# Another order and other operations in the opening of a two-block transformer kernel

## The reference, cut to what matters

```python
def rmsnorm(x, g):                       # x * rsqrt(mean(x*x) + eps) * g
...
cos, sin = rope_tables(positions)        # angle = position * inv (8 frequencies)
cond = jax.nn.silu(c)                    # 1 x 1024
for l in range(DEPTH):
    mod = (cond @ ada_w[l] + ada_b[l])[:, None, :]        # 1 x 6144
    sh1, sc1, g1, sh2, sc2, g2 = jnp.split(mod, 6, axis=-1)
    h = rmsnorm(x, norm1_g[l]) * (1 + sc1) + sh1
    x = x + g1 * hybrid_mixer(h, cos, sin, w_in[l], b_in[l], rel_bias[l], ...)   # first: h @ w_in + b_in
    h = rmsnorm(x, norm2_g[l]) * (1 + sc2) + sh2
    x = x + g2 * swiglu(h, w_ffn_in[l], w_ffn_out[l])
```

## Time and profile before

| | us |
|---|---|
| median of 3 runs (lowest, highest) | 1459.61 (1456.82, 1460.19) |
| the profiled execution | 1456.65 |
| its span, first to last instruction | 1454.8 |
| PE busy | 1432.1 (98%) |
| POOL busy | 1210.1 (83%) |
| ACT busy | 755.6 (52%) |
| DVE busy | 723.9 (50%) |

### The profile page before, as it was taken

One profiled execution on the slowest core, in us unless ns is written; L12 is line 12 of the kernel. 1 busy time (PEld: TensorE's weight loads), 2 busy tenths in 40 slices (PEclk: granted clock), 3 DMA queues, 4 the chain that ended last, 5 costly groups with the idle time before them and its releaser, 6 DMA issues.

```text
span 1454.8 us, 21549 instructions
## 1 busy us (share of the span) xinstructions
PE 1432.1 (98%) x7600; PEld 1199.7 (82%) x7600; DVE 723.9 (50%) x1557; ACT 755.6 (52%) x1272; POOL 1210.1 (83%) x984
## 2 busy tenths in 40 slices
PE   7999999999999999999999999999999999999997
PEld 5898777799988987778888888778888888788886
DVE  7863654766643754745566304454650044655202
ACT  4435774644444445765544445674654346655431
POOL 3899989888878986559898997966999977789994
PEclk9999999999999999999999999999999999999999
DMA  9994547689875996337676565644566755456651
GB/s 362 402 354 159 199 168 225 230 292 327 313 265 168 401 319 200 117 99 232 219 242 201 187 204 169 191 142 145 189 195 197 222 162 181 131 164 198 199 197 52
DMA packets 149415, 313.35 MB, mean 215 GB/s; under 512 B 10918, under 2 KB 31802, under 8 KB 149307
## 3 DMA queue, kind: packets, MB, share of 16 engines
q1 hardware_dynamic: 147552, 310.62, 63.8%
q10 hardware_dynamic: 1756, 1.35, 0.3%
HBM read 310.87 MB, written 1.06 MB: 214 GB/s over the span
## 4 chain that ended last, share of the span: by engine, by line
PE 92%; DVE 4%; ACT 1%; POOL 1%; DMA 1%; issue 1%; SPq 0%; DVEq 0%; ACTq 0%
PE bank L789 58%; PE bank L834 12%; PE bank L835 8%; PE bank L832 5%; PE bank L997 1%; PE bank L981 1%; POOL lo_units L733 1%; PE bank L870 1%; PE bank L967 1%; DMA x_rows<-in_x 1%; PE bank L1078 1%; PE bank L1013 1%; PE bank L1049 1%; PE bank L1039 0%; PE bank L1092 0%
## 5 line engine op out<-in xcount | busy, mean ns | idle before, releaser
L733 POOL TENSOR_TENSOR lo_units<-raw_units,hi_units 128x512 fp32r<-128x512 f32 (+3 forms) x928 | 1151.4, 1276 | 221.7 <-ACT hi_units L1371 220.6
L1371 ACT ACTIVATE hi_units<-raw_units 128x1024 fp32r<-128x1024 f32 (+1 forms) x470 | 482.6, 1030 | 411.1 <-PE bank L789 251.9
L789 PE MATMUL bank<-hi_units,turned 128*128 128x512 f32 (+3 forms) x1600 | 441.2, 390 | 1.2 <-DVE turned L1897 0.7
L789 PEld LDWEIGHTS bank<-hi_units,turned 128*128 128x128 f32 x1600 | 291.7, 189 | 53.5 <-issue 3.3
L835 PE MATMUL bank<-turned,lo_units 128*128 128x256 f32 x1024 | 288.0, 281 | 0.0
L789 PE MATMUL bank<-hi_units,turned_wide 128*128 128x512 f32 x992 | 274.5, 391 | 0.0
L834 PE MATMUL bank<-turned,hi_units 128*128 128x512 f32 x736 | 259.2, 397 | 0.0
L789 PE MATMUL bank<-lo_units,turned 128*128 128x512 f32 (+3 forms) x800 | 252.8, 383 | 0.9 <-POOL lo_units L733 0.5
L789 PEld LDWEIGHTS bank<-hi_units,turned_wide 128*128 128x128 f32 x992 | 185.3, 188 | 38.4 <-issue 0.5
L835 PEld LDWEIGHTS bank<-turned,lo_units 128*128 128x128 f32 x1024 | 194.4, 190 | 0.2
L789 PEld LDWEIGHTS bank<-lo_units,turned 128*128 128x128 f32 x800 | 149.7, 188 | 30.6 <-POOL lo_units L733 3.7
(11 more groups left out here) (261 smaller groups left out, 1288.6 us busy)
## 6 DMA issues: line engine op xcount, KB each, us to landing
ada_units<-in_ada_w SPq DMA_DIRECT2D x88, 512.0 KB, 7.8
raw_units<-in_w_ffn_tiles SPq DMA_DIRECT2D x72, 512.0 KB, 5.2
raw_units<-in_mlp_w_out SPq DMA_DIRECT2D x64, 512.0 KB, 3.3
raw_units<-in_mlp_w_tiles SPq DMA_DIRECT2D x56, 512.0 KB, 3.2
raw_units<-in_w_in SPq DMA_DIRECT2D x56, 458.0 KB, 9.7
raw_units<-in_w_in SPq DMA_DIRECT2D x48, 512.0 KB, 6.9
raw_units<-in_w_ffn_out SPq DMA_DIRECT2D x44, 512.0 KB, 3.5
raw_units<-in_moba_w_qkv SPq DMA_DIRECT2D x24, 512.0 KB, 3.7
```

The source lines that it names most:

```text
L733: pool.tensor_tensor(LO[:, s, b, 0:w], RAW[:, u["slot"], b, 0:w], HI_[:, s, b, 0:w].bitcast(F32), ALU.subtract).then_inc(lo_ready.sem, lo_ ...
L789: ins = pe.matmul(BANK[2 * c["pair"] + t][:, 0:w], (A[a] if A is BT else A[:, a])[:, part, t * P:(t + 1) * P], W[:, s, b, 0:w], start=(i = ...
L1371: act.activation(HI_[:, s, 0:n, 0:w], RAW[:, u["slot"], 0:n, 0:w], ACT.Copy)\
```

## The change

- The gain row and the whole bias row are brought first on ACT's queue, and one function, `constant_columns`, turns both into 24 columns by 24 one-column matmuls at the very start of TensorE's list. ACT copies them to SBUF (L1692 in the new numbering), ahead of its table load and of the squares. No tile is cleared any more, and DVE's sums of three chunks start by a plain multiply.
- `angles()` moves to the front of DVE's list, ahead of the first sums, and both sines to the front of ACT's, ahead of that copy. `tables()` moves ahead of `first_columns(0)`, and the issue of `rel_scratch` behind `first_hi(0)`.
- Unit 1 of shift 0 (chunk 0) leaves DVE too. It and unit 1 of scale 1 (chunk 3) are multiplied with the column of `cond` as the stationary operand and 512 columns moving, which gives a row (`sum_row`); ACT copies the row (`keep_sum_row`), and `column_sums` adds it by 4 more one-column matmuls.
- DVE makes the gained scale in `scale_columns` ahead of the reciprocal, so that only one addition is left between the sums of the shift and their use.
- The k-tiles of the first products go through ACT and DVE singly, and TensorE starts on each of them alone (`first_unit`).
- One unit, c1's unit 1, moves ahead of the sums of shift 1, and two fillers follow those sums.

TensorE's list from its start: in the kernel before,

The core of the diff; the removed lines of these functions stand in the kernel before, above, and the functions that are new are whole but for `first_turn` (the eight transposes of a half in one go) and `keep_sum_row` (one copy of a row of 512 by ACT):

```diff
-PE_UNITS = {(0, 3, 1)}
+PE_UNITS = {(0, 0, 1), (0, 3, 1)}
...
+        def constant_columns():
+            pe.wait_ge(first_gain_in, 16)
+            pe.wait_ge(first_bias_in, 16)
+            for j in range(3 * KT):
+                row = BIAS_ROW[:, j * P:(j + 1) * P] if j < 2 * KT else GAIN_ROW[:, (j - 2 * KT) * P:(j - 2 * KT + 1) * P]
+                ins = pe.matmul(columns[:, j:j + 1], row, ONES[0:1, 0:1], start=j == 0, stop=j == 3 * KT - 1)
+            ins.then_inc(product.sem, product.mark("constant columns"))
+        def sum_row(c, i, bank):
             u = c["units"][i]
             pe.wait_ge(ada_in[u["home"]][u["slot"]], 16 * (u["turn"] + 1))
             for k in range(UNIT_K):
+                kt = i * UNIT_K + k
+                ins = pe.matmul(bank[0:1, :], COND[:, kt:kt + 1], ada_raw(u)[:, k, :], start=k == 0, stop=k == UNIT_K - 1)
             ins.then_inc(ada_multiplied.sem, ada_multiplied.mark(u["index"]))
         def column_sums(c):
             n, half = c["key"][2], c["key"][2] % 2
             at = (KT if n >= 2 else 0) + 4 * half
             pe.wait_ge(ada_used.sem, ada_used.at(c["units"][-1]["index"]))
+            if n in SUM_ROW:
+                pe.wait_ge(act_side.sem, act_side.at(("sum row", n)))
+            if n < 2:
+                pe.wait_ge(rows.sem, rows.at(("scales", half)))
             for j in range(4):
+                if n in SUM_ROW:
+                    pe.matmul(columns[:, at + j:at + j + 1], SUM_ROW[n][:, j * P:(j + 1) * P], ONES[0:1, 0:1], start=j == 0, stop=False)
                 ins = pe.matmul(columns[:, at + j:at + j + 1], MOD[:, n * CW + j * P:n * CW + (j + 1) * P], ONES[:, 0:1],
+                                start=n not in SUM_ROW and j == 0, stop=j == 3)
+            ins.then_inc(product.sem, product.mark(("columns", n)))
...
+        def first_unit(c, i):
+            for m in range(UNIT_K):
+                pe.wait_ge(turned_lo.sem, turned_lo.at((("n1", 0), i * UNIT_K + m)))
+                unit(c, i, HT, only=m)
...
+        constant_columns()
         pe.wait_ge(ada_in[scale0["units"][0]["home"]][scale0["units"][0]["slot"]], 16)
+        keep_running(2)
+        pe.wait_ge(act_side.sem, act_side.at("constant columns"))
+        column_sums(scale0)
         keep_running(1)
+        sum_row(shift0, 1, BANK[2])
         for l in range(DEPTH):
             if l == 0:
                 tag = ("n1", l)
                 c0, c1 = todo.pop(0), todo.pop(0)
+                first_turn(0)
                 keep_running(1)
                 column_sums(shift0)
                 keep_running(2)
+                first_unit(c0, 0)
+                first_unit(c0, 1)
+                sum_row(scale1, 1, BANK[3])
+                first_turn(1)
+                column_sums(scale1)
                 unit(c1, 0, HT)
+                unit(c1, 1, HT)
                 column_sums(shift1)
+                keep_running(2, BANK[SB_[0]])
+                first_unit(c0, 2)
+                first_unit(c0, 3)
+                unit(c1, 2, HT)
+                unit(c1, 3, HT)
...
+            whole(b)
+            hi(a, rows)
+            hi(b, act_side)
+            hi(c, rows)
+            act.wait_ge(turned_lo.sem, turned_lo.at((("n1", 0), b)))
+            whole(d)
+            hi(d, act_side)
...
+        act.dma_start(GAIN_ROW, dram["norm1_g"][0:1, :]).then_inc(first_gain_in, 16)
+        act.dma_start(BIAS_ROW, dram["ada_b"][0:1, 0:4 * CW]).then_inc(first_bias_in, 16)
         act.dma_start(POS[:, :], dram["positions"].rearrange("b (t p) -> (b p) t", p=P),
                       allow_slow_non_contiguous=True).then_inc(pos_in, 16)
         act.wait_ge(c_in, 16)
         act.activation(CT, COND, ACT.Tanh, scale=0.5).then_inc(act_side.sem, act_side.mark("cond"))
+        act.dma_start(RB[:, :], dram["rel_bias"].rearrange("l h r -> (l h) r")).then_inc(rel_in, 16)
+        for what, dst in (("sin", SIN), ("cos", COS)):
+            act.wait_ge(rows.sem, rows.at(what))
+            act.activation(dst, dst, ACT.Sin).then_inc(act_side.sem, act_side.mark(what))
+        act.wait_ge(product.sem, product.at("constant columns"))
+        act.activation(MX[:, 0:3 * KT], BANK[SB_[1]][:, 0:3 * KT], ACT.Copy).then_inc(act_side.sem, act_side.mark("constant columns"))
         act.wait_ge(const_in, 16)
         bring_root_table(("n1", 0))
...
         unit_rows(0)
+        keep_sum_row(0, 1, BANK[2])
         unit_rows(1)
         prep(2)
         for l in range(DEPTH):
             if l == 0:
                 first_hi(0)
+                act.wait_ge(rows.sem, rows.at("rel"))
+                act.dma_start(scratch[:, :], RE[:, :]).then_inc(scratch_in, 16)
+                prep(3)
+                keep_sum_row(3, 1, BANK[3])
                 prep(NH)
                 first_hi(1)
                 prep(NH + 3)
...
+        def scale_columns(half):
+            columns, cols = BANK[SB_[1]], slice(4 * half, 4 * half + 4)
+            at = slice(KT + 4 * half, KT + 4 * half + 4)
+            dve.wait_ge(act_side.sem, act_side.at("constant columns"))
+            dve.wait_ge(product.sem, product.at(("columns", 2 + half)))
+            link(v.scalar_tensor_tensor(GAINED[:, cols], columns[:, at], 1.0, BIAS[:, at], ALU.add, ALU.add))
+            say(v.tensor_tensor(GAINED[:, cols], GAINED[:, cols], GAIN[:, cols], ALU.mult), ("scales", half))
...
+            say(v.tensor_tensor(SHIFT[:, cols], columns[:, cols], BIAS[:, cols], ALU.add), ("columns", half))
+            dve.wait_ge(turned.sem, turned.at((("n1", 0), half)))
+            whole(a)
+            lo(a)
+            lo(b)
+            whole(c)
+            lo(c)
+            lo(d)
...
+        angles()
         sums_upto(5)
+        scale_columns(0)
         dve.wait_ge(act_side.sem, act_side.at(("root", ("n1", 0))))
         say(v.reciprocal(RR[:, 0:NT], RSTD), "inverse root")
-        sums_upto(8)
+        sums_upto(7)
+        tables()
         for l in range(DEPTH):
             if l == 0:
                 first_columns(0)
-                sums_upto(15)
+                sums_upto(13)
+                scale_columns(1)
+                sums_upto(14)
                 first_columns(1)
-                tables()
-                angles()
```

More of the change, by code:

```diff
@@ L1200, in column_sums, with first_turn @@
-            if n < 2:
-                ins.then_inc(product.sem, product.mark(("columns", half)))
-        def keep_running(n):
+                                start=n not in SUM_ROW and j == 0, stop=j == 3)
+            ins.then_inc(product.sem, product.mark(("columns", n)))
+        def first_turn(half):
+            pe.wait_ge(act_side.sem, act_side.at(("unit rows", half)))
+            if half:
+                for k in (2, 3):
+                    pe.wait_ge(turned_lo.sem, turned_lo.at((("n1", 0), k)))
+            for k in range(4 * half, 4 * half + 4):
+                for t in range(NT):
+                    at = k % 4 // 2 * S + t * P
+                    ins = pe.transpose(BANK[(TQ, TP)[k % 2]][:, at:at + P], O[:, t, k * P:(k + 1) * P], con("ident"))
+            ins.then_inc(turned.sem, turned.mark((("n1", 0), half)))
@@ L1221, in _ @@
                 c0, c1 = todo.pop(0), todo.pop(0)
-                ready = lambda g: (act_side, ("unit rows", g // 2))
-                turn(tag, O, range(4), 0, ready)
-                turn(tag, O, range(4), 1, ready)
+                first_turn(0)
                 keep_running(1)
@@ L1932, in first_columns @@
[L1932 to L1938 removed]
+            a, b, c, d = range(4 * half, 4 * half + 4)
+            raw = lambda k: BANK[(TQ, TP)[k % 2]][:, k % 4 // 2 * S:(k % 4 // 2 + 1) * S]
```

101 lines of the change are left out of this document (23 added, 78 removed).

## The result

The changed kernel takes 1463.34 us (median of 6 runs, 1462.60 to 1464.30); the kernel before took 1459.37 beside it (6 runs, 1456.82 to 1460.99). The medians are 4.0 us apart, a quotient of 1.0027; the ratio on record, which isn't the quotient of the medians, is 1.0033 with an interval of 1.0021 to 1.0044. Either way the changed kernel is slower, by 4 to 5 us. The forecast was 1463.5.

A forecast was written before the change was run, and what follows sets the result against it. TensorE, busy 98% of the span, was taken to bound the kernel behind 52.19 us, a chain of waits the opening; 3.4 + 0.85 - 0.3 = +3.95 us on the median 1459.61 gave 1463.5, range 1458.0 to 1468.5.

The forecast's parts named there:

- The constant columns: Start of TensorE's list: 48 slow passes, 10.5 us, hold up ACT; the reciprocal ends at 20.3, 4.6 us later.
- Rival C: Opening: the column passes turn fast under way, end near 10 us and cost no wait; -1.4 us, 1458.2; chance 0.10.
- Rival B: Opening: the clock rises later, so scale 0's sums, a filler and much of the row sum take double; +5.5 to +7; chance 0.22.
- Who comes last: Ahead of the sums of shift 0: TensorE comes last at 24.35, DVE's last sum ends at 23.45; 0.9 us apart.
- First product: End of the opening on TensorE: the first product comes at 28.0 us, 3.4 later than before.
- The sums of shift 0: TensorE ahead of the first product: 16 passes instead of half as many, 1.8 to 1.95 us, ending at 26.2.
- The hand-over: From the sums of shift 0 to the first product: 1.85 us with single k-tiles instead of 3.06, saving 1.2.
- From the first product to the third chunk: TensorE's stretch up to the third column chunk: 28.4 us against 27.55, 0.85 later; bounds -1.0 and +2.0.
- The wait at c0's unit 3: Ahead of the third chunk: TensorE waits for ACT's rounding of weights; 0.8 us together with POOL's subtraction.
- The term of -0.3: Behind 52.19 us: TensorE's wait of about 0.3 us for POOL's remainders goes.
- What costs nothing: DVE's opening: the twelve operations of the angles take 2.5 us, hidden under the constant columns and the fillers.
- Rival D: Opening: POOL's first subtractions come 5 us later, and a wait of 3.3 for weights reaches TensorE; +7.3, 1466.9; chance 0.10.

The follow-up runs named there:

- shift_unit_on_dve: The changed kernel with unit 1 of shift 0 summed by DVE again, without its row sum on TensorE; 1464.77 us, ratio 1.0039.
- copy_late: The changed kernel with ACT's copy of the columns behind the root, and DVE's reciprocal and sums ahead of its scale columns; 1465.59 us, ratio 1.0045.
- before_again: The kernel before, run again with no edit; 1459.77 us, ratio 1.0002.
- one_constant: The changed kernel with one matmul of 24 columns in place of the 24 one-column matmuls, leaving gain and bias out; 1461.03 us, ratio 1.0020.
- filler_first: The changed kernel with the first two fillers ahead of the constant columns; 1468.34 us, ratio 1.0060.
- rows_only: The kernel before with both units as row sums and the sums of scale 1 ahead of c1's unit 0; 1461.24 us, ratio 1.0007.
- more_fillers: The kernel before with one more filler behind the sums of scale 0 and one more ahead of those of shift 0; 1457.66 us, ratio 0.9994.
- split_constants: The changed kernel with twelve of the constant columns at the start and twelve behind the first four products; 1466.67 us, ratio 1.0048.

## Why the prediction was right, and which terms were off

The total (+3.95 forecast, +4.0 between medians) and the sign hold, and so does the mechanism up to the first product. The stretch behind it was mis-sized beyond its own bounds, and the total came out by luck. Taken step by step:

- **The constant columns.** Right within 0.2 us: 48 passes from 4.39 to 14.69 (4.2 to 14.7 forecast), squares at 16.41 (16.5), fillers to 18.26 (18.3), sums of scale 0 to 19.63 (19.6), reciprocal to 20.34 (20.3). Rival C is refuted: 10.3 us of passes without a pause stayed at 0.216 us each. This disagrees with the rule of the Trainium skill, "TensorE: Matmul & The Clock Gate", Part 1, that the warm-up is a budget of time and not a number of matmuls. The prediction took these times from the trace and not from that page. Rival B did not come in the changed kernel's two profiles; in `shift_unit_on_dve`, whose list is the same up to there, one execution shows part of it (the filler behind the sums takes 2.05 and the transposes 1.97, where the changed kernel has 1.10 and 1.09).
- **Who comes last.** "It is TensorE and no longer DVE that comes last, by 0.9": by 0.73 in the trace (DVE done at 23.49, TensorE there at 24.22), and shown by `copy_late`, where DVE's reciprocal comes 3.8 us earlier and TensorE gains nothing by it. `shift_unit_on_dve` shows how near DVE is: with two sums more it is the last.
- **First product.** 28.0 forecast, 28.63 and 28.24 measured. Two terms were short. The sums of shift 0 were priced like sixteen passes of one kind (1.9); here matmuls of line 1197 and of line 1198, of two passes each, take turns, and a pass starts every 0.155 us, so they take 2.4. The hand-over took 2.0 (26.63 to 28.63) instead of 1.85.
- **From the first product to the third chunk.** This is the mis-sized term: 28.4 forecast, 31.07 measured, so 3.5 us more than before where 0.85 was forecast and +2.0 was the upper bound. The sums of scale 1 are the same kind of passes (2.4 instead of 1.9), and right behind them the clock fell: 0.59 over 39.07 to 43.20, so that c1's two units took 6.63 instead of 5.0. The wait at c0's unit 3 was forecast at 0.8 together with POOL and is 0.50 in TensorE's timeline, with 0.4 more inside the product behind it. A fall of the clock at that place stood in no term and no rival; B has it only ahead of the first product.
- **Why the total came out all the same.** Against the profiled execution before, the terms measured +3.99 to the first product, +3.52 to the third chunk and -0.91 behind it, 6.6 in all (forecast: +3.4, +0.85 and -0.3). The sum was made against an execution of the kernel before that had had little of this: its own clock fell for 3.4 us only the earlier trace rows, where `before_again` shows two longer stretches and a third chunk at 57.01. The prediction carried the difference to the median over as a constant (2.96) and so assumed that the changed kernel would be as lucky. It wasn't (+6.6 between the profiles), and the two errors, 2.65 in the terms and 2.7 in the base, cancel. That is luck and no merit of the sum. The term of -0.3 can't be tested by single profiles: in the fourteen of this study the stretch behind the third chunk takes 1400.9 to 1406.2 us.
- **What costs nothing.** The angles took 2.6 us from 5.93 (2.5 forecast) and were hidden. Rival D did not come: no transfer of weights is waited for by TensorE up to 61 us.

How the 4 us divide among the parts is not settled. Rows alone are at 1.0007, single k-tiles with and without the angles at 1.0007 and 1.0010, all within measuring error; the whole without its 48 passes is at 1.0020, the whole at 1.0033 and 1.0030. The parts aren't independent, because each shifts where the clock falls. The constant columns alone in the kernel before were not run. Also open is why the 1400 us behind the third chunk vary by themselves: they took 1402.6 and 1405.9 in two profiles of the kernel before, a difference as large as the terms disputed here; TensorE is busy 2.1 us longer there for the same 7404 passes, at a granted clock of 1.00.

## What to carry to other kernels

In an opening where TensorE's clock still changes, price a pass by the level at that place, and look at more than one profile before believing a single fall or its absence. Matmuls of one column are dear at the low level: a pass costs about 0.22 us, whether it goes over one row or over 128.

Whether a row of them also lets the clock fall is not shown. In the changed kernel, `copy_late`, `one_constant` and `filler_first` what ran behind sixteen or more was slow again. But other rows of this length had no fall behind them: sixteen passes at 24.22 in the changed kernel, sixteen at 32.17 and sixteen at 36.56 in the kernel before, sixteen at 37.96 in `filler_first`, and 24 at 36.02 in `rows_only`, whose clock stays at 1.00 from 22 to 60 us. And in seven of the fourteen profiles a fall begins between 38 and 40 us, among them `more_fillers`, where products at the high level stand right ahead of it.

Work moved from DVE to TensorE pays only where DVE is last; as soon as the list of TensorE itself makes the chain, take passes out of it, and look at the clock again: in `one_constant` and `split_constants` the time won by fewer passes was lost to the low level.

## What the runs showed of the hardware

- The granted clock fell without a pause of TensorE: behind 32 passes of one column in `filler_first` (0.13 us each, then 0.22), and at 39 us of the changed kernel behind sixteen (clock 0.59 for 4.1 us). Other rows of sixteen, in the same kernels, were followed by no fall; what lets it fall is open.
- The same four filler passes were followed by the high level in some kernels (the changed one, `before_again`: next passes 0.12 to 0.17) and not in others (`split_constants`, `one_constant`: 0.23), where they started 5.1 and 8.5 us earlier than in the changed one and a pause stood behind them. Which of the two mattered was not tested.
- One-column passes start every 0.155 us at the high level where matmuls over one row and over 128 rows take turns (16 from 24.22 to 26.63), and every 0.10 to 0.12 where all are of one kind (8 from 45.70 to 46.51 in the changed kernel, 8 from 30.50 to 31.48 in `more_fillers`).
